# Expert weights as 16 KB rows, 2 MB a transfer, with the contraction index permuted

## The chip, the cores and the metric

The kernel runs on one core of a Trainium2 chip. The metric is the device time of one execution in microseconds. A matmul runs on TensorE (PE in the profile), its weight loads are PEld; VectorE is DVE, ScalarE is ACT, GpSimd is POOL, and SyncE is SP, which issues nearly all transfers. A transfer is carried out by 16 DMA engines, each of which serves eight of the 128 partitions.

## The reference, cut to what matters

Two transformer blocks over 256 tokens of width 1024, in float32. The first has an attention and then a mixture of 32 experts, of which each token takes four; the second is a dense block. The change lies in the experts:

```python
def moe(h, router_w, router_b, w1, b1, w2, b2):
    logits = (h @ router_w + router_b).astype(jnp.float32)
    top_v, top_i = lax.top_k(logits, TOP_K)
    gates = jax.nn.softmax(top_v, axis=-1).astype(h.dtype)
    ...
    def expert_block(args):
        xb, e = args
        hid = xb @ w1[e] + b1[e]
        return clamped_swiglu(hid[:, :D_FF], hid[:, D_FF:]) @ w2[e] + b2[e]
```

`w1[e]` is 1024 x 2048 (8 MB), `w2[e]` is 1024 x 1024 (4 MB): 384 MB of weights for 32 experts, each read once.

## The kernel before

**Stages.** Loads and projections, attention, output projection and router run up to about 270 us. Then comes the expert stage, and from about 1245 us the second block.

**Experts in pairs.** `CAP` = 64 tokens of an expert are gathered at a time, and two experts share TensorE's 128 output rows: `mine(i)` is rows 0 to 63 or 64 to 127. There are 16 pairs, in a hardware loop on every engine. TensorE does in a pair, in this order (`hidden`, `gather`, `pe_rest`):

- the first weight: for k = 0 to 7 a contraction tile of 128 rows, four banks of 512 columns and two experts (L531; the profile shows each float32 matmul as two, so 16 of them a k), the bias rows b1 behind k = 5 (L540);
- the gather for the next pair (L519), a product of the tokens `hf` with a selection matrix; ScalarE copies its result to `gathered` (L602);
- four transposes of each half of the activated hidden values (L548), which ScalarE copies to `actT` (L615). Before them VectorE clips the values, multiplies (L650) and multiplies by the sigmoid (L654), 512 columns at a time;
- the second weight: j = 0 to 3, two contraction tiles each (L568), the bias rows b2 behind j = 2 (L577);
- the mix back to the tokens, four products (L588) that VectorE adds to `x2` (L669).

**The ring.** All large weights pass through `ring`, 12 slots of 1 MB (128 partitions of 8 KB). SP's program is one order of chunks written out by hand: the front's 38 chunks, then for each pair the list `PAIR`: 16 chunks of `w1` (for each k one of each expert) and 8 chunks of `w2` (for each j one of each). A chunk of `w1` is 128 consecutive rows, one row of 8 KB to a partition; a chunk of `w2` is 256 rows, two rows of 4 KB to a partition, 128 rows apart. SP waits until `ring_freed` shows that the chunk 12 places before has been used, and then issues (`pair_loads`, L495). TensorE raises `ring_freed` by two after each k and each j, and before each k and j it waits on `landed` of both slots (`pair_landed`). The ring is filled for the stage while attention and output projection run. If a chosen expert has more than 64 tokens, the same code runs further rounds (`OVER`).

Of the kernel before, what the change touches and what calls it, by code (L numbers as in the profile page):

```python
# [13 lines left out]
P = 128  # L14
# [42 lines left out]
FRONT = ADA0 + W_IN + MLA + ADA12 + W_OUT  # L57

PAIRS = E // 2
PAIR = [("w1", k, i) for k in range(KD) for i in range(2)] + [("w2", j, i) for j in range(4) for i in range(2)]  # L60
N_FRONT = len(FRONT)
N_MOE = PAIRS * len(PAIR)
assert len(PAIR) == 2 * SLOTS
BACK = ([("w_in2", k) for k in range(KD)] + [("w_out2", j) for j in range(4)]
        + [("ff1", 0)] + [c for j in range(15) for c in (("ff1", j + 1), ("ff2", j))] + [("ff2", 15)]
        + [("w_ple", 0)] + [("gate", j) for j in range(4)])
# [13 lines left out]
for _c, _n in CHUNK.items():  # L80
    if _n < N_BEFORE:
        SLOT_OF[_c], USE_OF[_c], AFTER[_c] = _n % SLOTS, _n // SLOTS + 1, _n - SLOTS + 1
    else:
        _m = _n - N_BEFORE
        _s, _last = FREED_BY_PAIR[_m % BACK_SLOTS]
        SLOT_OF[_c], USE_OF[_c] = _s, _last // SLOTS + 1 + _m // BACK_SLOTS + 1
        AFTER[_c] = _last + 1


# [80 lines left out]
def build(nc, a, out):  # L170
    with ExitStack() as ctx:
# [97 lines left out]
        out2 = o[:, 0, :]  # L269
        gs = mrows[:, 1:3, :].rearrange("p a n -> p (a n)")  # L270
        us = o[:, 1, :]
        sg = sq[:]
        actT = dq[:].rearrange("p a (j s) -> p (a j) s", j=4)

# [139 lines left out]
            pe.wait_ge(sem("w_split"), n + 1)  # L414
            return (w_hi[:, n % ROUNDED, :].bitcast(F32R), w_lo[:, SLOT_OF[chunk], :].bitcast(F32R))

        def source(kind, k, expert=None):

            if kind[:3] == "ada":
                t = int(kind[3])  # L420
                return a["w_ada"][0, k * P:(k + 1) * P, t * SLOT:(t + 1) * SLOT], slice(0, SLOT), None
            if kind == "w_in":
                return a["w_in"][0, k * P:(k + 1) * P, :], slice(0, IN_COLS), None
            if kind == "w_uq":
                return a["w_uq"][0].rearrange("(k p) n -> p k n", p=P), slice(0, 2 * 768), 2
            if kind == "w_ukv":
                return a["w_ukv"][0], slice(0, 1024), None
            if kind == "w1":
                return a["w1"][0, expert, k * P:(k + 1) * P, :], slice(0, SLOT), None
            if kind == "w2":  # L430
                return (a["w2"][0, expert, k * 2 * P:(k + 1) * 2 * P, :].rearrange("(k p) n -> p k n", p=P),
                        slice(0, SLOT), 2)
            if kind == "w_in2":
                return a["w_in_2"][0, k * P:(k + 1) * P, :], slice(0, IN2), None
            if kind == "ff1":
                return a["w_ff1_2"][0, :, k * 256:(k + 1) * 256].rearrange("(k p) n -> p k n", p=P), slice(0, SLOT), KD
            pairs = {"w_out2": "w_out_2", "ff2": "w_ff2_2", "w_ple": "w_ple_2", "gate": "w_ple_gate_2"}
            if kind in pairs:
                return (a[pairs[kind]][0, k * 2 * P:(k + 1) * 2 * P, :].rearrange("(k p) n -> p k n", p=P),
                        slice(0, SLOT), 2)  # L440
            if kind == "w_out":
                return a["w_out"][0, k * 2 * P:(k + 1) * 2 * P, :].rearrange("(k p) n -> p k n", p=P), slice(0, SLOT), 2
# [29 lines left out]

        def freed_by(n, i, which):

            return n * len(PAIR) + ((N_FRONT if which == MAIN else SLOTS) + i + 1)

        def pair_slot(i):
            return (N_FRONT + i) % SLOTS

        def load_most(eng):  # L480

# [2 lines left out]

        def pair_loads(sp, n, pair, which):

            for i, (kind, k, second) in enumerate(PAIR):
                src, cols, parts = source(kind, k, pair * 2 + second)
                s = pair_slot(i)
                dst = ring[:, s, cols]  # L490
                if parts:
                    dst = dst.rearrange("p (k n) -> p k n", k=parts)
                sp.wait_ge(moe("ring_freed", which),
                           n * len(PAIR) + ((N_FRONT if which == MAIN else SLOTS) + i + 1 - SLOTS))
                sp.dma_start(dst, src).then_inc(moe(f"landed{s}", which), 16)  # L495

        def sp_overflow(sp):
            count_ = load_most(sp)
# [5 lines left out]
                            pair_loads(sp, pair + (r - 1) * PAIRS, pair, OVER)  # L504
                        sp.wait_ge(moe("ring_freed", OVER), SLOTS + r * N_MOE)

        def pair_landed(pe, n, i, which):

            before = (N_FRONT + i) // SLOTS if which == MAIN else i // SLOTS
            pe.wait_ge(moe(f"landed{pair_slot(i)}", which), (n * 2 + (before + 1)) * 16)  # L510

        def gather(pe, n, which, y_read):

# [9 lines left out]
        def hidden(pe, n, which):  # L523

            pe.wait_ge(moe("xt_read", which), n + 1)
            for k in range(KD):
                for i in range(2):
                    pair_landed(pe, n, 2 * k + i, which)
                for q, bank_no in enumerate(GATE_BANKS + UP_BANKS):
                    for i in range(2):  # L530
                        m = pe.matmul(banks[bank_no][mine(i), :], gathered[:, k, mine(i)],  # L531
                                      ring[:, pair_slot(2 * k + i), q * 512:(q + 1) * 512],
                                      start=k == 0, stop=k == KD - 1, skip_group_check=True)
                    if k == KD - 1 and q == 1:
                        m.then_inc(moe("gate_full", which), 1)
                m.then_inc(moe("ring_freed", which), 2)
                if k == 5:
                    pe.wait_ge(moe("b1_in", which), (n + 1) * 16)
                    for q, bank_no in enumerate(GATE_BANKS + UP_BANKS):
                        m = pe.matmul(banks[bank_no][:], pick, b1rows[:, q * 512:(q + 1) * 512],  # L540
                                      start=False, stop=False, skip_group_check=True)

        def pe_rest(pe, n, which, ahead):
            for half in range(2):

                pe.wait_ge(moe("gated", which), n * 2 + (half + 1))
                for j in range(4):
                    m = pe.transpose(banks[TURN_BANKS[half]][:, j * P:(j + 1) * P],  # L548
                                     us[:, half * 512 + j * P:half * 512 + (j + 1) * P], ident[:])
                m.then_inc(moe("turned", which), 1)  # L550
                if half == 0:

# [2 lines left out]
                        m = pe.transpose(banks[SHARE_BANK][:, t * P:(t + 1) * P], selg[:, t, :], ident[:])  # L555
                    m.then_inc(moe("share_full", which), 1)

            for j in range(4):
                if j % 2 == 0:
                    pe.wait_ge(moe("act_read", which), n * 2 + (j // 2 + 1))  # L560
                for i in range(2):
                    pair_landed(pe, n, 2 * KD + 2 * j + i, which)
                for c in range(2):
                    for kk in range(2):
                        for i in range(2):
                            w = ring[:, pair_slot(2 * KD + 2 * j + i), :].rearrange("p (k n) -> p k n", k=2)
                            k = 2 * j + kk
                            m = pe.matmul(banks[OUT_BANKS[c]][mine(i), :], actT[:, k, mine(i)],  # L568
                                          w[:, kk, c * 512:(c + 1) * 512],
                                          start=k == 0, stop=k == KD - 1, skip_group_check=True)  # L570
                    if j == 3 and c == 0:
                        m.then_inc(moe("out_half", which), 1)
                m.then_inc(moe("ring_freed", which), 2)
                if j == 2:
                    pe.wait_ge(moe("b2_in", which), (n + 1) * 16)
                    for c in range(2):
                        pe.matmul(banks[OUT_BANKS[c]][:], pick, b2rows[:, c * 512:(c + 1) * 512],  # L577
                                  start=False, stop=False, skip_group_check=True)
# [50 lines left out]
        def dve_pair(dve, n, pair, which):  # L629
# [16 lines left out]
            for half in range(2):  # L646
# [4 lines left out]
                                         op0=ALU.add, op1=ALU.mult).then_inc(moe("up_gate", which), 1)  # L651
                dve.wait_ge(moe("up_gate", which), n * 2 + (half + 1))
                dve.wait_ge(moe("sigmoid", which), n * 2 + (half + 1))
                dve.tensor_tensor(us[:, cols], us[:, cols], sg[:, cols], ALU.mult).then_inc(moe("gated", which), 1)  # L654

            for c in range(2):
                if c == 0:
                    dve.wait_ge(moe("out_half", which), n + 1)
                else:
                    dve.wait_ge(moe("ring_freed", which), freed_by(n, len(PAIR) - 1, which))  # L660
                cols = slice(c * 512, c * 512 + 512)
                dve.tensor_tensor(out2[:, cols], banks[OUT_BANKS[c]][:], gf[:, cols], ALU.mult)\  # L662
                    .then_inc(moe("out_read", which), 1)
# [29 lines left out]
        def _(pool):  # L693
# [10 lines left out]
                    pool.dma_start(mrows[i:97 + i:32, t, :], src).then_inc(sem("bada_in" if t else "bada0_in"), 16)  # L704
            pool.dma_start(rb[:], a["router_b"]).then_inc(sem("router_in"), 16)
            wait_read(pool, "mixT0")
            pool.dma_start(rw, a["router_w"][0].rearrange("(k p) e -> p k e", p=P)).then_inc(sem("router_in"), 16)
            pool.wait_ge(sem("x1_done"), 4)
            step(pool.memset(below, 1.0))

# [260 lines left out]
        def _(dve):  # L971
# [202 lines left out]
            for t in range(NT):  # L1174
# [12 lines left out]
                step(V.reciprocal(stat[:, 6 + t:7 + t], stat[:, 4 + t:5 + t]))  # L1187
                for n in range(2):
                    cols = slice(n * 512, n * 512 + 512)
                    step(V.scalar_tensor_tensor(out=hf[:, t, cols], in0=xc[:, 2 + t, cols], scalar=stat[:, 6 + t:7 + t],  # L1190
                                                in1=bc[:, 2, cols], op0=ALU.mult, op1=ALU.mult))
                    step(V.tensor_tensor(hf[:, t, cols], hf[:, t, cols], bc[:, 1, cols], ALU.add), "hf_done")


            dve.wait_ge(sem("iota_done"), 1)
# [700 lines left out]
```

## Time and profile before

| | |
|---|---|
| median of 3 runs | 1600.18 us (1595.45 to 1604.42) |
| profiled execution | span 1596.0 us from the first to the last instruction; its own time outside the profile is not listed |
| TensorE matmul | busy 1472.8 us, 92% of the span |
| VectorE, ScalarE | 489.0 and 302.4 us |
| moved by DMA | 499.62 MB, 313 GB/s over the span |
| chain that ended last | PE 70%, DMA 17%, DVE 7%, ACT 3% |
| mean granted TensorE clock | 0.939 |

A busy share is an average over stages that have different limits. The chain of waits follows the work that ended last back in time, at each step to what released it, and shows for a stretch which engine set the time. DMA lines with "ring<-in_w" are the expert weights.

### The profile page before, as it was taken

Reading aid. Unit: us, or ns where it says so; the run is one execution under the profiler, and the core shown is the slowest. Engines: PE = TensorE matmul, PEld = TensorE weight load, DVE = VectorE, ACT = ScalarE, POOL = GpSimd, SP = SyncE. Lnnn points to the kernel's source line nnn. Section 1 sums busy time; section 2 is a strip of 40 time slices with the busy share of each in tenths; the row PEclk is TensorE's granted clock in tenths of the full one; section 3 lists DMA queues with packets and bytes.
Section 4 is the critical chain, followed back from the end, with each engine's and each line's share of the span. In section 5 each row is a group of like instructions: output and inputs, shape, how many; then the busy total and the mean of one; then the engine's idle time right before and its main releaser. Section 6 shows DMA issues by size and latency. Waiting matters only on the chain.

```text
span 1596.0 us, 18351 instructions
## 1 busy us (share of the span) xinstructions
PE 1472.8 (92%) x6832; PEld 764.0 (48%) x6832; DVE 489.0 (31%) x896; ACT 302.4 (19%) x445; POOL 15.6 (1%) x34
## 2 busy tenths in 40 slices
PE   4997987999999999999999999999999778899996
PEld 2764455433333333333333333333333567799985
DVE  1645434112112112112112111111211546655564
ACT  3414222101101101101001001001001344444441
POOL 1000001000000000000000000000000000000000
PEclk8999897999999999999999999999999877899998
DMA  9217905999999999999999999999999431465520
GB/s 375 100 49 316 416 7 188 366 419 417 416 419 417 415 421 417 415 421 416 415 420 416 416 420 416 414 421 411 408 420 348 158 130 38 164 195 185 185 106 27
DMA packets 106650, 499.62 MB, mean 313 GB/s; under 512 B 9272, under 2 KB 25688, under 8 KB 70736
## 3 DMA queue, kind: packets, MB, share of 16 engines
q1 hardware_dynamic: 103504, 492.86, 77.4%
q0 software_dynamic: 1648, 5.04, 1.0%
q10 hardware_dynamic: 1456, 1.16, 0.2%
q8 instruction: 26, 0.43, 0.1%
q14 instruction: 16, 0.13, 0.0%
HBM read 497.98 MB, written 1.05 MB: 313 GB/s over the span
## 4 chain that ended last, share of the span: by engine, by line
PE 70%; DMA 17%; DVE 7%; ACT 3%; issue 2%; SPq 1%; ACTq 0%; PEldq 0%; DVEq 0%
PE bank L1383 25%; PE bank L531 18%; DMA ring<-in_w 15%; PE bank L568 14%; PE bank L519 4%; PE bank L540 4%; PE bank L577 2%; DMA ring<-in_w_ada 2%; PE bank L588 1%; DVE w_lo L408 1%; ACT xn L602 1%; ACT xn L823 1%; ACT dq L615 1%; PE bank L1679 0%; ACT w_hi L401 0%
## 5 line engine op out<-in xcount | busy, mean ns | idle before, releaser
L531 PE MATMUL bank<-ring,xn 128*64 128x512 f32 x2048 | 480.7, 627 | 21.6 <-DMA ring<-in_w 20.1
L531 PEld LDWEIGHTS bank<-ring,xn 128*64 128x64 f32 x2048 | 154.7, 144 | 347.1 <-issue 347.1
L568 PE MATMUL bank<-ring,dq 128*64 128x512 f32 x1024 | 226.8, 595 | 9.2 <-ACT dq L615 9.2
L639 DVE TENSOR_SCALAR mrows<-bank 128x512 f32<-128x512 f32 x32 | 20.6, 686 | 500.2 <-PE bank L531 500.2
L610 ACT ACTIVATE sq<-mrows 128x512 f32<-128x512 f32 x32 | 19.6, 630 | 813.0 <-DVE mrows L639 813.0
L568 PEld LDWEIGHTS bank<-ring,dq 128*64 128x64 f32 x1024 | 70.6, 137 | 153.1 <-issue 140.1
L408 DVE TENSOR_TENSOR w_lo<-ring,w_hi 128x2048 fp32r<-128x2048 f32 (+1 forms) x48 | 103.2, 2158 | 42.7 <-ACT w_hi L401 42.4
L662 DVE TENSOR_TENSOR dk<-bank,bc 128x512 f32<-128x512 f32 x32 | 22.1, 691 | 269.0 <-PE bank L568 269.0
L401 ACT ACTIVATE w_hi<-ring 128x2048 fp32r<-128x2048 f32 (+1 forms) x48 | 85.9, 1802 | 33.7 <-PE bank L1383 33.6
L1383 PE MATMUL bank<-x_hi,w_hi 128*128 128x256 f32 x256 | 73.2, 286 | 1.8 <-DVE h_lo L1261 1.8
L1383 PE MATMUL bank<-h_lo,w_hi 128*128 128x256 f32 x256 | 73.1, 285 | 0.0
L1383 PE MATMUL bank<-x_hi,w_lo 128*128 128x256 f32 x256 | 73.0, 285 | 0.0
L519 PEld LDWEIGHTS bank<-xn 128*128 128x128 f32 x544 | 64.2, 197 | 15.2 <-issue 15.2
L519 PE MATMUL bank<-xn 128*128 128x128 f32 x544 | 67.5, 284 | 2.1 <-DVE xn L625 2.1
L540 PE MATMUL bank<-dv,small 2*128 2x512 f32 x128 | 64.2, 642 | 0.0
L588 PE MATMUL bank<-dk,xn 128*128 128x512 f32 x128 | 62.3, 620 | 0.0
L1383 PE MATMUL bank<-ring,hT 128*128 128x512 f32 (+2 forms) x120 | 52.6, 590 | 1.8 <-DVE hT L1008 1.8
L1383 PEld LDWEIGHTS bank<-x_hi,w_hi 128*128 128x128 f32 x256 | 49.8, 194 | 2.7 <-issue 2.2
L1383 PEld LDWEIGHTS bank<-h_lo,w_hi 128*128 128x128 f32 x256 | 49.8, 194 | 0.6
L1383 PE MATMUL bank<-w_hi,wide_hi 128*128 128x512 f32 x128 | 50.0, 391 | 0.0
L1383 PE MATMUL bank<-w_lo,wide_hi 128*128 128x512 f32 x128 | 50.0, 390 | 0.0
L1383 PE MATMUL bank<-w_hi,wide_lo 128*128 128x512 f32 x128 | 49.8, 389 | 0.0
(331 smaller groups left out, 1485.2 us busy)
## 6 DMA issues: line engine op xcount, KB each, us to landing
ring<-in_w SPq DMA_DIRECT2D x384, 1024.0 KB, 19.6
ring<-in_w_ff SPq DMA_DIRECT2D x32, 1024.0 KB, 5.3
ring<-in_w_ada SPq DMA_DIRECT2D x24, 1024.0 KB, 17.1
ring<-in_w_out SPq DMA_DIRECT2D x8, 1024.0 KB, 8.5
ring<-in_w_in SPq DMA_DIRECT2D x8, 992.0 KB, 26.6
ring<-in_w_in SPq DMA_DIRECT2D x8, 640.0 KB, 12.2
ring<-in_w_ple_gate SPq DMA_DIRECT2D x4, 1024.0 KB, 4.8
xc<-in_ctx SPq DMA_DIRECT2D x1, 1024.0 KB, 5.0
```

The costliest lines, as they stand in the source:

```text
L401: act.activation(w_hi[:, n % ROUNDED, 0:w].bitcast(F32R), slot(chunk)[:, 0:w], ACT.Copy)\
L408: dve.tensor_tensor(w_lo[:, SLOT_OF[chunk], 0:w].bitcast(F32R), slot(chunk)[:, 0:w], w_hi[:, n % ROUNDED, 0:w], ALU.subtract).then_inc(sem ...
L519: m = pe.matmul(banks[GATHER_BANKS[k // 4]][:, k % 4 * P:(k % 4 + 1) * P], hf[:, t, k * P:(k + 1) * P], sel[:, t, :], start=t == 0, stop=t ...
L531: m = pe.matmul(banks[bank_no][mine(i), :], gathered[:, k, mine(i)], ring[:, pair_slot(2 * k + i), q * 512:(q + 1) * 512], start=k == 0, s ...
L540: m = pe.matmul(banks[bank_no][:], pick, b1rows[:, q * 512:(q + 1) * 512], start=False, stop=False, skip_group_check=True)
L568: m = pe.matmul(banks[OUT_BANKS[c]][mine(i), :], actT[:, k, mine(i)], w[:, kk, c * 512:(c + 1) * 512], start=k == 0, stop=k == KD - 1, ski ...
L577: pe.matmul(banks[OUT_BANKS[c]][:], pick, b2rows[:, c * 512:(c + 1) * 512], start=False, stop=False, skip_group_check=True)
L588: pe.matmul(banks[MIX_BANKS[c]][:], selgT[:, t * P:(t + 1) * P], out2[:, c * 512:(c + 1) * 512], start=True, stop=True, skip_group_check=T ...
L610: act.activation(sg[:, cols], gs[:, cols], ACT.Sigmoid, scale=ALPHA).then_inc(moe("sigmoid", which), 1)
L639: dve.tensor_scalar(gs[:, half * 512:half * 512 + 512], banks[GATE_BANKS[half]][:], LIMIT, None, ALU.min)\
L662: dve.tensor_tensor(out2[:, cols], banks[OUT_BANKS[c]][:], gf[:, cols], ALU.mult)\
L1383: return pe.matmul(out_, lhsT, rhs, start=first, stop=last, skip_group_check=True)
```

## The change

Contraction tiles no longer hold 128 consecutive rows of a weight. For `w1`, partition p of a block takes rows 2p and 2p + 1 of 256 consecutive ones, which lie side by side in memory: one run of 16 KB. For `w2`, it takes rows 4p to 4p + 3 of 512: again 16 KB. A block is 2 MB and fills two neighbouring slots, so a pair has 12 transfers for 24. Tile k of the first product then contracts over every second row of a block of 256, and tile k of the second over every fourth of 512. The other operand follows: `hf` is written with its columns reordered within 256 (`by_twos`, at L1192; the product before it goes to `sq` first), the router's weight is loaded in the same order, and VectorE's last multiply (L654) reads the hidden values and the sigmoid at a step of four and writes `act_rows`, so that the transposes read 128 columns in a row. Two slots are waited for together (`block_landed`) before k = 0, 2, 4, 6 and before each half of the second weight, and `ring_freed` goes up by four after k = 1, 3, 5, 7 and after each half. The bias rows b2 stand behind the first half instead of behind three quarters. `b1`, the columns of the first product and the order of the output are untouched.

```diff
-PAIR = [("w1", k, i) for k in range(KD) for i in range(2)] + [("w2", j, i) for j in range(4) for i in range(2)]
+PAIR_BLOCKS = [("w1", k, i) for k in range(4) for i in range(2)] + [("w2", j, i) for j in range(2) for i in range(2)]
+PAIR_CHUNKS = 2 * len(PAIR_BLOCKS)
 N_FRONT = len(FRONT)
-N_MOE = PAIRS * len(PAIR)
-assert len(PAIR) == 2 * SLOTS
+N_MOE = PAIRS * PAIR_CHUNKS
+assert PAIR_CHUNKS == 2 * SLOTS
...
+        act_rows = gs.rearrange("p (k s) -> p k s", k=KD)
...
+        def by_twos(x, turned=False):
+
+            if turned:
+                return x.rearrange("p (k r s) -> p k r s", k=2, r=2)
+            return x.rearrange("p (k s r) -> p k r s", k=2, r=2)
+
+        def by_fours(x):
+
+            return x.rearrange("p (s r) -> p r s", r=4)
 
...
-            for i, (kind, k, second) in enumerate(PAIR):
-                src, cols, parts = source(kind, k, pair * 2 + second)
-                s = pair_slot(i)
-                dst = ring[:, s, cols]
-                if parts:
-                    dst = dst.rearrange("p (k n) -> p k n", k=parts)
+            for i, (kind, k, second) in enumerate(PAIR_BLOCKS):
+                expert = pair * 2 + second
+                if kind == "w1":
+                    src = a["w1"][0, expert, k * 2 * P:(k + 1) * 2 * P, :].rearrange("(p r) n -> p (r n)", p=P)
+                else:
+                    src = a["w2"][0, expert, k * 4 * P:(k + 1) * 4 * P, :].rearrange("(p r) n -> p (r n)", p=P)
+                s = block_slot(i)
                 sp.wait_ge(moe("ring_freed", which),
-                           n * len(PAIR) + ((N_FRONT if which == MAIN else SLOTS) + i + 1 - SLOTS))
-                sp.dma_start(dst, src).then_inc(moe(f"landed{s}", which), 16)
+                           n * PAIR_CHUNKS + ((N_FRONT if which == MAIN else SLOTS) + 2 * i + 2 - SLOTS))
+                sp.dma_start(ring[:, s:s + 2, :].rearrange("p a n -> p (a n)"), src)\
+                    .then_inc(moe(f"block_landed{s // 2}", which), 16)
...
+        def block_landed(pe, n, i, which):
+
+            pe.wait_ge(moe(f"block_landed{block_slot(i) // 2}", which), (n * 2 + (2 * i // SLOTS + 1)) * 16)
+
+        def rows_of(i, rows):
+
+            s = block_slot(i)
+            return ring[:, s:s + 2, :].rearrange("p a n -> p (a n)").rearrange("p (r n) -> p r n", r=rows)
...
-                    pair_landed(pe, n, 2 * k + i, which)
+                at = k // 2 * 2
+                if k % 2 == 0:
+                    for i in range(2):
+                        block_landed(pe, n, at + i, which)
                 for q, bank_no in enumerate(GATE_BANKS + UP_BANKS):
                     for i in range(2):
                         m = pe.matmul(banks[bank_no][mine(i), :], gathered[:, k, mine(i)],
-                                      ring[:, pair_slot(2 * k + i), q * 512:(q + 1) * 512],
+                                      rows_of(at + i, 2)[:, k % 2, q * 512:(q + 1) * 512],
                                       start=k == 0, stop=k == KD - 1, skip_group_check=True)
                     if k == KD - 1 and q == 1:
                         m.then_inc(moe("gate_full", which), 1)
-                m.then_inc(moe("ring_freed", which), 2)
+                if k % 2 == 1:
+                    m.then_inc(moe("ring_freed", which), 4)
...
-            for j in range(4):
-                if j % 2 == 0:
-                    pe.wait_ge(moe("act_read", which), n * 2 + (j // 2 + 1))
+            for j in range(2):
+                pe.wait_ge(moe("act_read", which), n * 2 + (j + 1))
                 for i in range(2):
-                    pair_landed(pe, n, 2 * KD + 2 * j + i, which)
+                    block_landed(pe, n, 8 + 2 * j + i, which)
                 for c in range(2):
-                    for kk in range(2):
+                    for r in range(4):
                         for i in range(2):
-                            w = ring[:, pair_slot(2 * KD + 2 * j + i), :].rearrange("p (k n) -> p k n", k=2)
-                            k = 2 * j + kk
+                            k = 4 * j + r
                             m = pe.matmul(banks[OUT_BANKS[c]][mine(i), :], actT[:, k, mine(i)],
-                                          w[:, kk, c * 512:(c + 1) * 512],
+                                          rows_of(8 + 2 * j + i, 4)[:, r, c * 512:(c + 1) * 512],
                                           start=k == 0, stop=k == KD - 1, skip_group_check=True)
-                    if j == 3 and c == 0:
+                    if j == 1 and c == 0:
                         m.then_inc(moe("out_half", which), 1)
-                m.then_inc(moe("ring_freed", which), 2)
-                if j == 2:
+                m.then_inc(moe("ring_freed", which), 4)
+                if j == 0:
...
-                dve.tensor_tensor(us[:, cols], us[:, cols], sg[:, cols], ALU.mult).then_inc(moe("gated", which), 1)
+                dve.tensor_tensor(act_rows[:, half * 4:half * 4 + 4, :], by_fours(us[:, cols]), by_fours(sg[:, cols]), ALU.mult)\
+                    .then_inc(moe("gated", which), 1)
...
-            pool.dma_start(rw, a["router_w"][0].rearrange("(k p) e -> p k e", p=P)).then_inc(sem("router_in"), 16)
+            pool.dma_start(rw.rearrange("p (k r) e -> p k r e", r=2), a["router_w"][0].rearrange("(k p r) e -> p k r e", p=P, r=2)).then_inc(sem("router_in"), 16)
...
-                    step(V.scalar_tensor_tensor(out=hf[:, t, cols], in0=xc[:, 2 + t, cols], scalar=stat[:, 6 + t:7 + t],
+                    step(V.scalar_tensor_tensor(out=sq[:, 0:512], in0=xc[:, 2 + t, cols], scalar=stat[:, 6 + t:7 + t],
                                                 in1=bc[:, 2, cols], op0=ALU.mult, op1=ALU.mult))
-                    step(V.tensor_tensor(hf[:, t, cols], hf[:, t, cols], bc[:, 1, cols], ALU.add), "hf_done")
+                    step(V.tensor_tensor(by_twos(hf[:, t, cols], True), by_twos(sq[:, 0:512]), by_twos(bc[:, 1, cols]),
+                                         ALU.add), "hf_done")
```

## Rows read from the trace of the kernel before

**Rows 1.** The page: DMA engines busy in tenths and GB/s, 40 slices of the span.
```profile
DMA  9217905999999999999999999999999431465520
GB/s 375 100 49 316 416 7 188 366 419 417 416 419 417 415 421 417 415 421 416 415 420 416 416 420 416 414 421 411 408 420 348 158 130 38 164 195 185 185 106 27
```

**Rows 2.** Chain of waits, pairs 0 to 3: start us, us, what.
```profile
278.69 20.82 PE bank L531 x96
...
303.14 8.71 PE bank L531 x32
...
317.29 10.52 PE bank L568 x48
...
333.30 3.83 PE bank L588 x8
337.13 7.88 PE bank L531 x36
...
395.44 20.75 PE bank L531 x96
...
455.45 4.87 PE bank L531 x21
```

**Rows 3.** Chain of waits, pair 5, pair 15 and the stage's end.
```profile
590.72 3.65 PE bank L531 x16
...
1177.55 24.21 DMA ring<-in_w
...
1201.90 3.65 PE bank L531 x16
...
1244.85 0.70 DVE xc L669
...
1259.38 29.43 PE bank L1383 x144
```

**Rows 4.** Windows: from:to us, length, busy by engine, granted clock, DMA share, GB/s.
```profile
297.00:309.00 12.00, 12.00 (x40) 3.99 (x38) 0.00 (x0) 0.00 (x0) 0.00 (x0) 0.86 1.02 409
358.00:370.00 12.00, 12.00 (x40) 3.75 (x39) 1.29 (x2) 0.77 (x2) 0.00 (x0) 0.86 1.03 410
419.00:431.00 12.00, 12.00 (x42) 3.73 (x41) 2.06 (x4) 1.23 (x2) 0.00 (x0) 0.72 1.03 410
318.00:350.00 32.00, 32.00 (x136) 10.29 (x134) 5.77 (x14) 1.28 (x1) 0.00 (x0) 1.00 1.01 421
379.00:411.00 32.00, 32.00 (x136) 10.41 (x134) 5.70 (x14) 0.00 (x0) 0.00 (x0) 1.00 1.01 421
440.00:472.00 32.00, 32.00 (x136) 10.40 (x134) 5.70 (x14) 0.00 (x0) 0.00 (x0) 1.00 1.01 422
```

**Rows 5.** Line L495, SP's issues: ns min/median/max; issue to landing.
```profile
L495 SPq DMA_DIRECT2D ring<-in_w x384: 332/333/4478, 165.6 to 1213.5; - x192
...
DMA to landing us min/median/max: 4.7/19.6/26.4
```

**Rows 6.** Window at the restart of the queue in pair 0.
```profile
283.00:288.00 5.00, 5.00 (x26) 2.07 (x24) 0.00 (x0) 0.00 (x0) 0.00 (x0) 1.00 0.85 333
```

**Rows 7.** Groups by line and form on VectorE: busy us, mean ns, idle before.
```profile
L654 DVE TENSOR_TENSOR dk<-dk,sq 128x512 f32<-128x512 f32 x32 | 22.1, 692 | 1.1
...
L1289 DVE TENSOR_REDUCE psum_sum<-dv 128x2 f32<-128x256 f32 x4 | 1.7, 420 | 0.1
...
L1210 DVE TENSOR_REDUCE chosen<-sq 128x64 f32<-128x256 f32 x1 | 0.6, 591 | 0.0
```

**Rows 8.** Timeline of VectorE and ScalarE in pair 0.
```profile
315.15 0.69 DVE L654 TENSOR_TENSOR dk<-dk,sq 128x512 f32<-128x512 f32 x1
...
315.80 0.27 ACTq L597 DMA_DIRECT2D xc<-in_b  x1
...
316.63 1.09 ACT L615 ACTIVATE dq<-bank 128x512 f32<-128x512 f32 x2
```

**Rows 9.** Chain of waits ahead of the router.
```profile
257.95 0.70 DVE xn L1192
```

More of the change, by code:

```diff
@@ L85 @@
         _s, _last = FREED_BY_PAIR[_m % BACK_SLOTS]
-        SLOT_OF[_c], USE_OF[_c] = _s, _last // SLOTS + 1 + _m // BACK_SLOTS + 1
+        SLOT_OF[_c], USE_OF[_c] = _s, len(range(_s, N_FRONT, SLOTS)) + _m // BACK_SLOTS + 1
         AFTER[_c] = _last + 1
@@ L415, in split_weights, with source @@
             return (w_hi[:, n % ROUNDED, :].bitcast(F32R), w_lo[:, SLOT_OF[chunk], :].bitcast(F32R))
-        def source(kind, k, expert=None):
+        def source(kind, k):
             if kind[:3] == "ada":
@@ L427, in source @@
                 return a["w_ukv"][0], slice(0, 1024), None
[L428 to L432, printed above, removed]
             if kind == "w_in2":
@@ L473, in freed_by, with block_slot @@
         def freed_by(n, i, which):
-            return n * len(PAIR) + ((N_FRONT if which == MAIN else SLOTS) + i + 1)
-        def pair_slot(i):
-            return (N_FRONT + i) % SLOTS
+            return n * PAIR_CHUNKS + ((N_FRONT if which == MAIN else SLOTS) + i + 1)
+        def block_slot(i):
+            return (N_FRONT + 2 * i) % SLOTS
+        def by_twos(x, turned=False):
[4 more added lines that the diff above has]
+            return x.rearrange("p (s r) -> p r s", r=4)
         def load_most(eng):
@@ L505, in sp_overflow @@
                         sp.wait_ge(moe("ring_freed", OVER), SLOTS + r * N_MOE)
-        def pair_landed(pe, n, i, which):
-            before = (N_FRONT + i) // SLOTS if which == MAIN else i // SLOTS
-            pe.wait_ge(moe(f"landed{pair_slot(i)}", which), (n * 2 + (before + 1)) * 16)
+        def block_landed(pe, n, i, which):
[3 more added lines that the diff above has]
+            return ring[:, s:s + 2, :].rearrange("p a n -> p (a n)").rearrange("p (r n) -> p r n", r=rows)
         def gather(pe, n, which, y_read):
@@ L526, in hidden @@
             for k in range(KD):
-                for i in range(2):
-                    pair_landed(pe, n, 2 * k + i, which)
+                at = k // 2 * 2
+                if k % 2 == 0:
+                    for i in range(2):
+                        block_landed(pe, n, at + i, which)
                 for q, bank_no in enumerate(GATE_BANKS + UP_BANKS):
@@ L548, in pe_rest @@
                     m = pe.transpose(banks[TURN_BANKS[half]][:, j * P:(j + 1) * P],
-                                     us[:, half * 512 + j * P:half * 512 + (j + 1) * P], ident[:])
+                                     act_rows[:, half * 4 + j, :], ident[:])
                 m.then_inc(moe("turned", which), 1)
@@ L659, in dve_pair @@
                 else:
-                    dve.wait_ge(moe("ring_freed", which), freed_by(n, len(PAIR) - 1, which))
+                    dve.wait_ge(moe("ring_freed", which), freed_by(n, PAIR_CHUNKS - 1, which))
                 cols = slice(c * 512, c * 512 + 512)
```

## Prediction

> **What bounds the kernel now.** The page comes first: over the slices of the expert stage (from about 280 to 1240 us) the DMA engines read 9 in tenths, mostly at 414 to 421 GB/s [rows 1], and TensorE is busy through whole stretches of 32 us as well [rows 4]. Shares that high do not say which one sets the end, so the chain of waits is read next. In the first pairs of experts it holds no DMA at all: pair 0 begins at 278.69 and pair 1 at 337.13 us, 58.4 us of TensorE work, fed from a ring that was full when the stage began [rows 2]. From pair 5 on the chain holds a long DMA piece in every pair (24.21 us in pair 15), and the matmuls behind it (k = 5 of the first weight) start at 590.72 in pair 5 and at 1201.90 in pair 15, which is 611.18 us for ten pairs, 61.12 each [rows 3]. So the ring's lead is used up by pair 5, and after that the weight stream sets the pace, with TensorE 2.7 us a pair behind it. What comes behind the last such wait is 1244.85 - 1201.90 = 42.95 us of TensorE [rows 3].
>
> The stream's rate depends on the length of its rows. Ring transfers keep their order, so a stretch of the stage holds one kind: 12 us of second-weight rows (4 KB) ran at 409, 410 and 410 GB/s, 32 us of first-weight rows (8 KB) at 421, 421 and 422 [rows 4]. In time of one engine of sixteen (mean rates 409.7 and 421.3) a 4 KB row takes 4096 x 16 / 409.7 = 160.0 ns and an 8 KB row 8192 x 16 / 421.3 = 311.1 ns. If both are a fixed part and a part by bytes, the fixed part is 2 x 160.0 - 311.1 = 8.9 ns a row.
>
> **What the change does to the stream.** Each pair has 128 rows of 8 KB and 128 of 4 KB per engine: 128 x (311.1 + 160.0) = 60.30 us. The measured 61.12 leaves 0.82 us a pair that the two rates don't hold (biases of the experts on the same engines, the engine that is slowest); I keep it. After, the same bytes are 96 rows of 16 KB per engine. No row of the trace shows one in this queue. By the fixed part a 16 KB row takes 2 x 311.1 - 8.9 = 613.3 ns, the bound from above is two 8 KB rows, 622.2, and the best pair of rates in the rows (409 and 422) gives 611.4. I take 613.3: 96 x 0.6133 + 0.82 = 59.70 us a pair, 1.42 less; the bounds are 60.55 and 59.52. From the refill's start to the last wait there are 15 pairs of stream (360 transfers of 1 MB): -21.3 us, bounds -8.6 and -24.0.
>
> Bytes by time between the two row lengths are 4096 / 151.1 ns, 27.1 GB/s an engine, 434 GB/s for sixteen. The Trainium skill (DMA: Bandwidth & Descriptors, Where 436 GB/s comes from) puts the ports' ceiling at 435.2 GB/s, and its section on small descriptors has a fixed overhead per packet; the trace agrees with the ceiling.
>
> Half as many transfers: nothing. An issue costs SP 0.33 us, 8 us for the 24 of a pair, and a transfer lands 19.6 us (median) after its issue although 1 MB passes every 2.55 us (61.12 / 24), so some eight transfers are queued and a start-up cost of each is covered by those ahead [rows 5]. The Trainium skill (DMA: Bandwidth & Descriptors, Anatomy of one DMA) fits 2.0 us + bytes / 436e3 to a single transfer, by which 192 transfers fewer would save 384 us. The 2.55 us for 1 MB is below that page's 4.4, so here the trace does not bear the fixed part out.
>
> **What coarser blocks cost.** Slots come free by fours, after two k, and a block is waited for as a whole.
> - Start: the ring is full when the stage begins. Between 283 and 288 us the queue moves 333 GB/s [rows 6]; at 421 that is 3.95 us of work, so it runs again from about 284, behind k = 0 of pair 0, which ends at 282. After, the first slots come free behind k = 1. One k is 20.82 / 6 = 3.47 us [rows 2], so the whole stream starts 3.5 us later, on the path: +3.5.
> - End: the last transfer that TensorE waits for (k = 5 before) is now in the block of k = 4 and 5, so both stand behind it: one k more, +3.5.
> - Between them: does the queue run dry? Count from the landing of the block of k = 4, 5, by the TensorE pieces of [rows 2]: blocks are freed at +7 (two k), +19 (3.6 us of bias, then 8.71 for k = 6, 7), +32 (5.4 to 317.29, then two thirds of 10.52), +41 (333.30), then behind the mix at +52 and +58 (k = 0, 1 and 2, 3 of the next pair; less a period, -8 and -1). The stream, at 9.95 us for four slots, wants them at +20, +30, +40, +50, and the last two at 0 and +10. The least room is 8 us, over three transfers of 1 MB. Cost 0; if a stall goes anywhere, it is TensorE's wait before k = 5, which moves to k = 4.
>
> **What the permutation costs.**
> - Transposes, matmuls, weight loads: the same number and shapes; runs of 512 columns stay contiguous. 0.
> - VectorE's last multiply of each half now reads two operands at a step of four elements. Before, it is 0.69 us [rows 7]. The nearest stepped row is the reduction at L1210, 591 ns for 256 elements against 420 for the unstepped one at L1289: 0.67 ns an element more [rows 7], so 0.34 us for 512. From above I bound it by twice the unstepped time, +0.69; below by 0. Who waits: the transposes of half 1, queued ahead of the second weight's matmuls. The multiply of half 1 ends at 315.84, some 0.16 us and 0.6 us of transposes follow, and the matmuls start at 317.29 because ScalarE's copy of half 0, begun at 316.63, holds them [rows 8]. That is 0.7 us of cover: +0.68 for two multiplies just fits; at the upper bound +0.7 a pair goes on TensorE, which has 59.70 - 58.4 = 1.3 us of cover by the stream. I take 0 inside the stream and +0.3 behind the last wait.
> - Ahead of the router, the addition at L1192 (0.70 us, twice on the chain for the second token tile, one of the two in [rows 9]) reads and writes at steps: +0.34 each by the same row, bounds 0 and +0.69: +0.7, before the stage begins.
> - b2's wait moves from behind three quarters of the second weight to behind half: 7 us after its start instead of 10.5. Its issue is at 315.80, 1.5 us before the start [rows 8]; 8 KB have 8.5 us. 0. The router weight's load in longer pieces lies under the attention: 0.
> - The second block's first weights get their slots up to 3.5 us later. 0: TensorE's next weight matmuls start at 1259.38, 14.5 us behind the stage [rows 3].
>
> **Sum.** -21.3 + 3.5 + 3.5 + 0.3 + 0.7 = -13.3 us. The profiled span is 1596.0 us, of which no separate time is given; the median of the runs is 1600.18, 4.2 above it, and I put the difference on the median: 1587 us, 0.8% faster.
>
> **Rivals.**
> 1. A 16 KB row costs two 8 KB rows (the fixed part is not per row, or long rows are cut in two). 60.55 a pair: -8.6 + 8.0 = -0.6, 1600 us. For it: no row of 16 KB in this queue. Against: the step from 4 to 8 KB paid. 0.14.
> 2. Rows of 16 KB run worse: they are cut into 4 KB pieces, or runs side by side in memory hinder each other, so that they go at the 4 KB rate. 96 x 640 ns + 0.82 = 62.26 a pair, +1.14 x 15 + 8.0 = +25, 1625 us. The place is the expert stream, the price 27 ns a row, and it decides from where a 16 KB row takes over 622.6 ns, since 15 x (61.12 - 60.59) pays the 8.0 of coarser blocks. Against: 8 KB rows, which would be cut too, run faster than 4 KB ones. 0.11. The Trainium skill (DMA: Bandwidth & Descriptors, Latency and other measured facts) warns of row pitches at large powers of two, from 512 KiB on; here the pitch goes to 16 KB, and no row here shows such a loss.
> 3. The stream gets ahead for good, as it would if the 0.82 us went too: 58.9 a pair leaves a ring whose lead lasts nearly to the end, and TensorE sets all 16 pairs: 278.69 + 16 x 58.4 = 1213 for 1244.85, -32, +1 for VectorE: 1569 us. For it: TensorE's 58.4 is 1.3 below the forecast pace. 0.10. A fixed cost per transfer, as in the fit of the Trainium skill's page named above, would lead here too.
> 4. TensorE takes over at a slower pace. The granted clock is 0.72 to 0.86, part of the time at 1.2 GHz, in stretches that hold TensorE's bias rows, and 1.00, all of it at 2.4 GHz, in others [rows 4]; a pair with such a stretch took 60.0 us (395.44 to 455.45, [rows 2]). If nearly all pairs were like that and the stepped multiply cost its upper bound, 60.3 a pair (a lag is made up in the next pair as long as the mean is below 59.7): -0.8 x 15 + 8 = -4, 1596 us. Against: most early pairs were at 58.4. 0.10.
>
> **How the numbers follow.** The forecast holds 0.55, its own range 1579 to 1594 (the bounds of the row time, the stepped operations, the scatter of the runs, 1595 to 1604). Rivals 3 and 2 together are 0.21 at the ends; the range is 1571 to 1604. About 0.5% (8 us) is what a measurement of this kernel can tell. Faster: 0.55 + 0.10 + 0.03 of rival 4, less 0.02 of the forecast's upper tail, 0.66. Same: 0.14 + 0.07 + 0.02 = 0.23. Slower: 0.11.
>
> **What would show it.** The stream at about 427 GB/s through the whole pair, without the steps of 410 and 421; DMA waits on the chain in front of k = 4, 59.7 us apart, from about pair 5 on again (7 us less of lead, drained by 1.3 a pair for 2.7); the queue's start 3.5 us later in pair 0; 46 us from the last wait to the end of the stage; the stepped multiplies at about 1.03 us and the gap to the second weight's first matmul as before. The prediction is wrong if the 16 KB rows show 421 or 410 GB/s, if the queue shows gaps inside a pair, if the waits vanish (rival 3), or if the chain has VectorE's L654 in it.

## The result, and the profile after

The changed kernel takes 1582.1 us (median of 4 runs, 1581.37 to 1583.51) for 1602.3 before (4 runs, 1595.45 to 1604.47): a ratio of 0.9894, 95% interval 0.9871 to 0.9916, so 1.1% faster. Beside further runs of both, later and on one chip, it was 0.9909 (0.9894 to 0.9925). The forecast was 1587 us, 0.8% faster. In the later rounds the kernel before had medians of 1598.36, 1597.13 and 1599.86 us over 24, 7 and 10 runs, so the 1602.3 of this comparison lies high and the gain is nearer 0.9% than 1.1%.

The page of the changed kernel: span, DMA in tenths and GB/s in 40 slices, the queue of the weights, and their issues.

```profile
span 1579.6 us, 17439 instructions
...
DMA  9217905799999999999999999999998531455530
GB/s 377 103 34 332 403 27 189 306 423 427 429 429 427 429 427 428 427 428 417 424 426 416 425 428 414 425 428 379 429 424 374 183 104 63 151 187 187 187 107 27
...
q1 hardware_dynamic: 59472, 492.85, 76.2%
...
ring<-in_w SPq DMA_DIRECT2D x192, 2048.0 KB, 16.3
```

In the expert stage the queue moves up to 429 GB/s where it moved up to 421 [rows 1]; the same bytes went in 59472 packets for 103504. A row of 16 KB goes as one packet: in one pair of a later run (bias_resident, 765.52 to 824.25 us) 12 transfers take 1728 packets, 144 each, which is 128 rows and 16 packets under 512 B. The windows that answer to [rows 4] and, in the last two lines, to [rows 6]:

```profile
379.00:411.00 32.00, 32.00 (x136) 10.43 (x134) 5.69 (x14) 0.00 (x0) 0.00 (x0) 1.00 1.00 427
440.00:472.00 32.00, 32.00 (x136) 10.37 (x134) 5.69 (x14) 0.00 (x0) 0.00 (x0) 1.00 1.01 429
297.00:309.00 12.00, 12.00 (x42) 4.08 (x40) 0.00 (x0) 0.00 (x0) 0.00 (x0) 0.86 1.01 430
358.00:370.00 12.00, 12.00 (x42) 4.01 (x40) 1.19 (x2) 0.46 (x1) 0.00 (x0) 0.86 1.01 429
283.00:288.00 5.00, 5.00 (x26) 1.93 (x23) 0.00 (x0) 0.00 (x0) 0.00 (x0) 1.00 0.24 49
286.00:291.00 5.00, 5.00 (x26) 1.93 (x23) 0.00 (x0) 0.00 (x0) 0.00 (x0) 1.00 0.79 269
```

The step between the two kinds of rows is gone: 427 to 430 GB/s in both. The queue starts later in pair 0: 269 GB/s over the last window is 3.1 us of work at 429, so it runs from about 287.9, 8.9 us behind the stage's first matmul. Before, by the same working, it ran from 284.05, 5.4 us behind.

The chain of waits of the changed kernel (start us, us, what): pairs 0 and 1, the first waits on the stream, the last one, and the stage's end.

```profile
278.93 20.82 PE bank L547 x96
...
337.39 20.75 PE bank L547 x96
...
527.30 7.09 PE bank L547 x32
...
567.26 19.57 DMA ring<-in_w
...
586.97 8.78 PE bank L547 x32
...
1064.52 8.79 PE bank L547 x32
...
1229.33 0.70 DVE xc L685
```

The matmuls behind a wait are now those of k = 4 and 5 (x32 for x16 in [rows 3]). From 527.30 to 1064.52 is nine pairs, 59.69 us each; before it was 61.12. TensorE alone takes 58.46 us a pair (278.93 to 337.39) for 58.44. The stage, from the first weight matmul to the last addition's start, takes 1229.33 - 278.93 = 950.4 us for 966.2 [rows 2, 3].

### The profile page after: what moved, and what is told of

The parts are those of the page before. It is cut to its first block, busy times and chain, and to the rows that moved or that the text cites. A ratio compares the mean times of both kernels' runs of the same rounds, so it can differ in the third digit from the quotient of the medians.

```text
span 1579.6 us, 17439 instructions
## 1 busy us (share of the span) xinstructions
PE 1460.2 (92%) x6832; PEld 764.6 (48%) x6832; DVE 501.9 (32%) x896; ACT 304.1 (19%) x445; POOL 15.5 (1%) x34
## 3 DMA queue, kind: packets, MB, share of 16 engines
q1 hardware_dynamic: 59472, 492.85, 76.2%
## 4 chain that ended last, share of the span: by engine, by line
PE 70%; DMA 13%; DVE 10%; issue 3%; ACT 2%; SPq 1%; PEldq 0%; DVEq 0%; ACTq 0%
PE bank L1400 25%; PE bank L547 21%; PE bank L583 14%; DMA ring<-in_w 12%; PE bank L557 4%; PE bank L592 2%; DMA ring<-in_w_ada 2%; PE bank L603 1%; DVE dk L665 1%; DVE mrows L669 1%; DVE w_lo L410 1%; DVE dk L659 1%; PE bank L565 1%; ACT xn L839 1%; PE bank L1696 0%
## 5 line engine op out<-in xcount | busy, mean ns | idle before, releaser
L547 PE MATMUL bank<-ring,xn 128*64 128x512 f32 x2048 | 468.9, 616 | 20.4 <-DMA ring<-in_w 19.0
L654 DVE TENSOR_SCALAR mrows<-bank 128x512 f32<-128x512 f32 x32 | 20.6, 686 | 484.2 <-PE bank L547 484.2
```

Of the source, the lines that this page charges most:

```text
L654: dve.tensor_scalar(gs[:, half * 512:half * 512 + 512], banks[GATE_BANKS[half]][:], LIMIT, None, ALU.min)\
```

## The experiments

Three theories. **Row length**: a row has a fixed part, so longer rows make the stream faster. **Transfer size**: a transfer has a fixed part, so fewer ones do. **Biases**: the 0.82 us a pair that the row rates did not explain belongs to the small loads of the experts' biases. The stage's length, from the first weight matmul to L669's (L685's) piece behind the last mix, and the pace, from wait to wait on the chain, are the measures. The stage's start is no measure: it lay between 274.7 and 283.4 us in programs whose front is alike, and this may be much of the scatter of the runs.

**Old rows in 2 MB transfers.** The changed kernel with the contraction index of before, in three places:

```diff
-src = a["w1"][0, expert, ...].rearrange("(p r) n -> p (r n)", p=P)
+src, parts = a["w1"][0, expert, ...].rearrange("(r p) n -> p r n", p=P), 2
-src = a["w2"][0, expert, ...].rearrange("(p r) n -> p (r n)", p=P)
+src, parts = a["w2"][0, expert, ...].rearrange("(r p) n -> p r n", p=P), 4
```

(and `by_twos`, `by_fours` and the router weight's load without the permutation.)

> The changed kernel with the contraction index as before: 12 transfers of 2 MB a pair and the coarse frees and waits, but rows of 8 KB (two a partition) and 4 KB (four a partition). If row length made the gain, DMA waits come 61.1 us apart and the expert stage takes 966 + 7 = 973 us, span about 1602, ratio to before 1.004. If the size of a transfer made it, pace 59.7, stage 950 us, span 1580, ratio 0.989.

Measured: ratio to before 1.0044 (1.0027 to 1.0060). Its windows at the places of the first weight (8 KB rows) and the second (4 KB), and its chain:

```profile
318.00:350.00 32.00, 32.00 (x136) 10.44 (x134) 5.76 (x14) 0.30 (x1) 0.00 (x0) 1.00 1.01 421
297.00:309.00 12.00, 12.00 (x42) 3.96 (x40) 0.00 (x0) 0.00 (x0) 0.00 (x0) 0.86 1.02 409
```

```profile
277.70 12.63 PE bank L550 x57
...
593.14 7.09 PE bank L550 x32
...
1205.21 7.09 PE bank L550 x32
...
1249.95 0.70 DVE xc L688
```

The rates are those of before, 421 and 409, in transfers twice as large. Ten pairs take 612.07 us, 61.21 each, and the stage 972.3 (it began at 277.70). The theory of transfer size falls: without the long rows the whole gain is gone, and 6 us more.

**Coarse frees and waits alone.** The kernel before, 24 transfers of 1 MB:

```diff
-                for i in range(2):
-                    pair_landed(pe, n, 2 * k + i, which)
+                if k % 2 == 0:
+                    for i in range(4):
+                        pair_landed(pe, n, 2 * k + i, which)
...
-                m.then_inc(moe("ring_freed", which), 2)
+                if k % 2 == 1:
+                    m.then_inc(moe("ring_freed", which), 4)
```

and so for the second weight.

> The kernel before with its 24 transfers of 1 MB and its rows, but frees by fours after every second k and waits for four chunks. If coarseness costs one k at the stage's start and one at its end, the stage takes 966 + 7 = 973 us at a pace of 61.1 and the run equals that of old_rows_2mb within 1 us. If the coarseness is free (the 8 us of room being all that counts), 966 us. If the queue runs dry between, the pace rises above 61.2 and GB/s dips inside pairs.

Measured: 1.0047 (1.0033 to 1.0062). The stage takes 972.7 us (283.40 to 1256.09), 0.4 us from the run above, in which the transfers were of 2 MB. Part of that closeness is luck: up to the last wait on the stream the two took 926.3 and 927.5 us, behind it 46.39 and 44.74, because TensorE went through the end at different clocks (a granted clock of 0.66 over 1220 to 1230 us here, 0.83 over 1215 to 1225 us there). To within these 1 to 2 us the size of a transfer gives nothing, of the 21.9 us that the rows give. Coarseness costs 6.5 us. Its chain at the end:

```profile
1209.70 7.09 PE bank L532 x32
...
1256.09 0.70 DVE xc L673
```

46.39 us lie behind the last wait for 42.95 before: one k more, +3.44. At the start the queue moves 313 GB/s between 291 and 296 us, 3.7 us of work at 421, so it runs again 8.9 us behind the first matmul for 5.4 before, +3.5. The two make 6.9, and the stage is 6.5 us longer.

**One weight at a time.** 16 KB rows for the first weight only, and for the second only, each with the old rows of the other in 2 MB transfers (and only that operand permuted which goes with the long rows):

```diff
# w1_long_only
-src = a["w2"][0, expert, ...].rearrange("(p r) n -> p (r n)", p=P)
+src, parts = a["w2"][0, expert, ...].rearrange("(r p) n -> p r n", p=P), 4
# w2_long_only
-src = a["w1"][0, expert, ...].rearrange("(p r) n -> p (r n)", p=P)
+src, parts = a["w1"][0, expert, ...].rearrange("(r p) n -> p r n", p=P), 2
```

> The changed kernel with 16 KB rows for the first weight only; the second weight in 2 MB transfers of 4 KB rows, the multiply unstepped. By row times (16 KB 611 ns, 8 KB 311, 4 KB 160) the first weight's rows save 0.7 us a pair and the second's 0.9: pace 61.1 - 0.7 = 60.4 to 60.5 us, stage 962 us. If a row has no fixed part and 4 KB rows alone are slow, pace 61.1 and stage 973.

> The changed kernel with 16 KB rows for the second weight only; the first in 2 MB transfers of 8 KB rows. By the row times pace 60.2 to 60.4 us, stage 960 us. If a row has no fixed part and only 4 KB rows are slow, all of the gain is here: pace 59.7, stage 950.

The chain of the run with a long first weight:

```profile
652.05 7.09 PE bank L550 x32
...
1197.68 8.62 PE bank L550 x32
...
1243.94 0.70 DVE xc L688
```

and of the run with a long second weight:

```profile
653.40 7.09 PE bank L550 x32
...
1196.06 7.09 PE bank L550 x32
...
1239.13 0.70 DVE xc L688
```

Nine pairs each: 60.63 and 60.30 us a pair, stages of 965.4 and 957.0 us (starts 278.54 and 282.11), ratios 0.9994 (0.9981 to 1.0007) and 0.9954 (0.9937 to 0.9970). Against 972.3 with neither, the first weight's rows save 6.9 us and the second's 15.3, together 22.2; with both it is 972.3 - 950.4 = 21.9. By pace it is 0.58 and 0.91 us a pair, together 1.49, and 61.21 - 59.69 = 1.52 with both. The parts add up either way. The paces were expected at 60.4 to 60.5 and 60.2 to 60.4, so the first weight's was missed by 0.1 to 0.2 us; the stages, expected at 962 and 960 us, missed by 3 us each way. The stage lengths hold more than the rows: behind the last wait lie 46.26 us in the first run, where k = 4 and 5 took 8.62 us, and 43.07 in the second, where they took 7.09. The pace is the cleaner measure. By it the second weight, where rows get four times as long, carries some 60% of the gain with one third of the bytes.

**The biases.** The loads of b1 and b2 taken out of the loop, so that every pair uses the biases of experts 0 and 1 and the other experts' are left out:

```diff
-            act.dma_start(b1rows, a["b1"][0, bass.ds(pair * 2, 2), :]).then_inc(moe("b1_in", which), 16)
+            if which == MAIN:
+                act.sem_inc(moe("b1_in", which), 16)
+                return
+            act.dma_start(b1rows, a["b1"][0, bass.ds(pair * 2, 2), :]).then_inc(moe("b1_in", which), 16)
```

and so for b2, in the changed kernel and in the one before.

> The changed kernel without the 32 small bias loads in the loop: the biases of experts 0 and 1 are loaded once ahead of the stage and used for every pair (the other experts' biases are left out). If those loads, one 8 KB and one 4 KB row a pair on an engine that streams weights too, are what lies between 58.7 and 59.7 us, the pace falls by 0.47 us to 59.2 or 59.3 and the stage by 7 us to 943. If the slowest engine is slow for another reason, 59.7 and 950.

> The kernel before with the same omission (biases of experts 0 and 1 for every pair). By the same theory pace 61.15 - 0.47 = 60.7 us and the stage 7 us shorter, 959; by the rival 61.15 and 966.

Measured: 0.9838 (0.9807 to 0.9869) for the changed kernel and 0.9914 (0.9880 to 0.9947) for the one before. The chain of the latter:

```profile
648.25 3.65 PE bank L531 x16
...
1130.33 3.65 PE bank L531 x16
...
1231.90 0.70 DVE xc L675
```

Eight pairs in 482.08 us, 60.26 each: what the two row times alone gave in the prediction, 60.30. The whole 0.82 was the biases. The stage takes 952.9 us (from 278.96) where 959 was expected. In the changed kernel no DMA wait is left on the chain in the stage, which takes 939.0 us (279.31 to 1218.29) where 943 was expected: TensorE sets nearly all of it.

The price was larger than the 0.47 us of one 8 KB and one 4 KB row that I had expected, so two more runs of the kernel before: with b1's loads only, and with each load issued twice (the copies to unused partitions).

```diff
+            act.dma_start(dv[32:34, :, :].rearrange("p t c -> p (t c)"), a["b1"][0, bass.ds(pair * 2, 2), :]).then_inc(moe("b1_in", which), 16)
```

> The kernel before with the b1 load of each pair kept and b2's taken out of the loop (one load ahead, the b2 of experts 0 and 1 for all pairs). Without both loads the pace was 60.3 us and with both 61.15. If the price goes by bytes, b1 has two thirds of 0.85: 60.85 to 60.9. If each load costs the same, 60.7. If it is the time of one row on one engine (0.31 us), 60.6.

> The kernel before with each bias load issued twice, the second to unused partitions. If the price adds up on the slowest engine, the pace goes from 61.15 to 62.0 us and the stage from 966 to about 979. If there is a price only for having a second queue in use at all, 61.15 to 61.3.

The chain of the first, and then of the second:

```profile
645.67 3.65 PE bank L531 x16
...
1193.11 3.65 PE bank L531 x16
```

```profile
599.32 3.65 PE bank L531 x16
...
1218.30 3.65 PE bank L531 x16
```

60.83 us a pair with b1 alone (nine pairs) and 61.90 with twice both (ten pairs), for 60.26 with none and 61.12 with both. So, in one trace of each, it goes by bytes and adds up: 0.57 for the 16 KB of b1, 0.86 for the 24 KB of both, 1.64 for twice both. Ratios: 0.9945 (0.9924 to 0.9967) and 1.0068 (1.0048 to 1.0089). It is 1.8 times the two rows' time on one engine, near the time of all four rows (2 x 0.47); which engine carries them the trace does not show, and this stays open. The bytes say that most engines are not held up. The weights of a pair are 25.17 MB. In the kernel before, with a wait at 590.72, 651.90, 713.05 and 774.29 us, the queue of the weights moved 25.51, 25.51 and 25.52 MB in the three pairs between. The 0.34 MB too much are 0.8 us at 417 GB/s: most engines run ahead, by just what the pace lacks. Without the bias loads it moved 25.17 MB in a pair (648.25 to 708.55 us). So a wait ends with the slowest engine or engines, and the mean rate of a window can lie above what the pace gives: 427 to 430 GB/s in the changed kernel, where 25.17 MB in 59.69 us are 421.6.

**The multiply without a step.** The changed kernel with `by_fours` taking its operand in order:

```diff
-            return x.rearrange("p (s r) -> p r s", r=4)
+            return x.rearrange("p (r s) -> p r s", r=4)
```

> The changed kernel with VectorE's last multiply reading its operands without a step (the hidden values go to the second product in the order of the kernel before, so they meet the wrong weight rows). The multiply takes 0.69 us for 1.10; TensorE's start of the second weight moves by 0.1 us at most, and the time stays within 1 us of the changed kernel's (span 1579.6), since two multiplies fit under ScalarE's copies. Rival: the chain has the multiply in every pair, so 0.4 to 0.8 us a pair in the pairs that no DMA wait holds (about six), 3 to 5 us less.

VectorE's forms in the changed kernel (busy us, mean ns, idle before), which answer to [rows 7]:

```profile
L669 DVE TENSOR_TENSOR mrows<-dk,sq 128x512 f32<-128x512 f32 x32 | 35.3, 1104 | 1.1
...
L1208 DVE TENSOR_TENSOR xn<-sq,bc 128x512 f32<-128x512 f32 x4 | 2.8, 695 | 0.1
```

With the step the multiply takes 1104 ns, without 692. The stage takes 949.8 us without it (281.67 to 1231.47) for 950.4, and its chain shows TensorE and ScalarE where the changed kernel's shows the two multiplies. The ratio, 0.9907 (0.9875 to 0.9939), is not below the changed kernel's. In pair 1 the second weight starts 5.49 us behind the end of k = 7 in the changed kernel (370.51 to 376.00), 5.44 without the step and 5.43 in the kernel before. So all but 0.05 us of the 0.41 is hidden by ScalarE's copies, as counted; that the chain names the multiply says only that it ended last of two that end nearly together.

**A version that beats both.** All 32 experts' biases loaded once, 384 KB on 32 partitions, and the pair chosen by the other operand of the bias product, 128 columns that ScalarE copies from a table GpSimd has made:

```diff
-            act.dma_start(b1rows, a["b1"][0, bass.ds(pair * 2, 2), :]).then_inc(moe("b1_in", which), 16)
+            act.activation(pick1, picks[:, bass.ds(pair * P, P)], ACT.Copy).then_inc(moe("b1_in", which), 1)
...
+            act.dma_start(b1all, a["b1"][0]).then_inc(sem("bias_in"), 16)
+            act.dma_start(b2all, a["b2"][0]).then_inc(sem("bias_in"), 16)
```

> The changed kernel with all 32 experts' biases loaded once, ahead of the stage, on 32 partitions; the bias rows of a pair come from a product of 32 rows with a selection that ScalarE copies (128 columns) where it issued the bias loads. If the bias loads are what slows the slowest engine, 59.2 or 59.3 us a pair and a span of about 1573, 0.4% below the changed kernel; the product has the same columns, so TensorE is unchanged. Rival: no change, 1580; or the two copies of 0.2 us on ScalarE delay the second weight by 0.2 us a pair, which the stream covers.

> The changed kernel itself, beside the next one on one chip. All theories: pace 59.7 us where a DMA wait holds it, stage 950 us, ratio 0.989 to 0.991.

> The kernel bias_resident once more, beside the changed kernel: 6 to 8 us less than after_again, stage 940 to 943 us, few DMA waits or none, and those 58.7 us apart.

Measured: 0.9840 (0.9806 to 0.9874), and beside the changed kernel, in five rounds on one chip, 1575.43 us for 1585.78: 0.9844 (0.9828 to 0.9860) and 0.9909 (0.9894 to 0.9925). In the first run two DMA waits are left on the chain, one pair apart:

```profile
765.52 7.09 PE bank L548 x32
...
824.25 7.09 PE bank L548 x32
```

58.73 us; if no small load is in it, that is 96 rows of 612 ns. The stages take 942.5 and 939.9 us (281.51 to 1223.96, 282.44 to 1222.34), 8 to 10 us less than the changed kernel's 950.4 and 949.6; stream and TensorE (58.4) are now 0.3 us a pair apart. The expectation had the bias loads at 0.47 us a pair and so the pace at 59.2 or 59.3; the span is 1575.4 us for the 1573 expected.

## Why the prediction was right, point by point

- **A 16 KB row at 613.3 ns, 59.70 us a pair.** Right: 59.69. Solved from the single runs, with 0.86 us for biases and 128 rows of the other kind at 160.0 ns (20.48 us) or 311.1 ns (39.82 us), a 16 KB row takes (60.63 - 0.86 - 20.48) / 64 = 614 ns for the first weight and (60.30 - 0.86 - 39.82) / 32 = 613 for the second; from bias_resident 612. Rival 1 (622.2) and rival 2 (640) are out, and so is its reason that long rows are cut: a row is one packet. The trace agrees with the ports' ceiling of 435.2 GB/s that the Trainium skill states (DMA: Bandwidth & Descriptors, Where 436 GB/s comes from): 430 is the highest of the windows of 12 and 32 us above. Slices of 1.5 us, as in the last fence below, scatter from 393 to 470 where the queue is full; one holds 2.5 rows of an engine.
- **Transfer size: nothing.** Right, to within 1 to 2 us, by 972.3 against 972.7 us. The Trainium skill's fit with 2.0 us a transfer (DMA: Bandwidth & Descriptors, Anatomy of one DMA) is for single transfers issued from GpSimd, and these are SP's; with some eight of them queued, 192 transfers fewer change the stage by no more than that. That the start-up is covered by the transfers ahead fits this, but no run shows it by itself.
- **Coarse blocks: +7.0.** Measured +6.5, half at the start and half at the end. In the changed kernel the queue started 3.8 us later, 3.6 of it against the stage's own start. No wait of pair 14 or 15 is on its chain, so its end was 1.0 us less than 2 x 59.7 + 46.4: 164.8 us from 1064.52 on.
- **Queue never dry between, 0.** Right for the time, not for the queue. In pair 13 of the changed kernel TensorE was late (bias rows of k = 5 in 4.99 us for 3.62, k = 6 and 7 in 9.02 for 8.74), and the queue all but stopped twice. The window from 1050 to 1110 us in 40 slices of 1.5 us:

```profile
GB/s 459 404 437 426 404 459 415 448 393 459 415 437 426 426 437 404 470 393 459 393 459 415 437 426 262 186 251 415 448 407 440 426 295 55 251 415 437 415 448 404
```

  Three slices at 186 to 262 and three at 55 to 295 GB/s. TensorE had fallen back at the lower clock: from 1066 to 1068 and from 1076 to 1082 us the granted clock was 0.50, which is 1.2 GHz. Smaller dips came earlier: the changed kernel's 40 slices hold 417, 416 and 414 GB/s beside 424 to 428, and each lies behind a pair whose k = 4 and 5 took 8.78 us (waits ending at 706.26, 825.74 and 945.15). (A fifth such pair, behind 586.97, shows no dip.) TensorE 1.7 to 3.3 us late does not use up the 8 us of room that were counted. That count takes the 16 engines as one; if most of them run ahead of the slowest, as the bytes under the biases suggest, they want their blocks earlier. No run shows this by itself. The dips cost nothing: the pace stayed at 59.69, and behind pair 13 no wait on the stream followed.
- **Stepped multiply: +0.34 each, hidden.** 0.41 each, and hidden but for 0.05 us.
- **Addition ahead of the router: +0.7.** This term failed: the addition takes 695 ns for 692. It reads at a step of two, and writes in order, not at a step as the prediction has it. The row it was sized by, L1210, is a reduction that reads at a step of 32 elements. That the same row came near for the step of four (0.67 ns an element for 0.80) is luck.
- **The 0.82 us kept.** Right to keep, and now it has a cause, the loads of the biases; only the way in which they cost it is open.
- **Rival 3**, TensorE setting all pairs at 1569, needed the 0.82 us to go too. It did not here; where it was taken away, the time went to 1574 to 1575.
- **Rival 4.** A pair at half clock in part (in another pair k = 4, 5 in 8.78 us for 7.09, with a granted clock of 0.73 from 708 to 712 us, part of it at 1.2 GHz) follows a long wait and falls into time that the stream sets; the pace did not move. Only in pair 13 did it put TensorE behind the stream.
- **The signs.** Two of the signs of being wrong came though the time was right: the queue has gaps, and the chain has the stepped multiply (L669 now), in pairs 0 and 1 among others. The first cost no time, the second at most 0.05 us a pair. The waits came from pair 4 on instead of 5, and none in pairs 14 and 15, so the 46 us behind the last wait stand only in coarse_1mb.

In sum -13.3 was forecast; the profiled span fell by 16.4. Of this the stage is 15.8 for 14.0 forecast: 1.0 at its end, where the stream no longer held TensorE, the 0.3 of the multiply, and 0.5 net in the pace (from the queue's restart to the last wait it was 61.19 before for 61.12 assumed, and 59.74 after for 59.70). Ahead of the stage 0.2 us were added for 0.7, which proves little as this start scatters by 8.7 us; behind the stage 0.9 us were saved for none, and no run shows why. The 1587 has 4.2 us between span and median in it; in every run on record the time lies 1.7 to 1.8 us above its span, so the rest was scatter of the runs.

## What to carry to other kernels

Where a stream of large loads sets the pace, compute the time of a row from two row lengths in the trace; if their difference in bytes already runs at the highest rate and the rest is a fixed part, longer rows give back just that part; larger transfers of the same rows gave nothing here, with some eight in the queue. Ask what else is on the same queues: 24 KB of small loads a pair cost 0.86 us, as much as the fixed part of 96 rows. A coarser ring cost one step of work at the stream's start and one at its end. Between them it cost no time here, though the queue had gaps that a count of the room for all 16 engines as one did not foresee. And where a wait is for the last of 16 engines, take the price of a small load from the pace between waits; the mean rate does not show it.

## What the runs showed of the hardware that was not expected

- Small loads on two partitions, issued from ScalarE beside a full stream, cost 1.8 times the time that their rows would take on one engine: 0.57 us for two rows of 8 KB, 0.86 with two of 4 KB besides, 1.64 for twice that. The other engines were not held up: the queue moved 25.51 MB a pair where the pace of the waits holds 25.17.
- VectorE's float32 addition of 128 x 512 elements with both operands read at a step of two, written in order: 695 ns, as without (692). The multiply with both operands read at a step of four: 1104 ns for 692, 0.80 ns an element more.
- The time at which the expert stage starts differs by up to 9 us between programs that are alike up to there.
